# The first group's projections between the latents' statistics and their broadcasts, in a hybrid MLA/SSD decoder layer

## What is computed

```python
h = rmsnorm(x, g_pre_mix)
h_q, h_kv, h_pe, z, xbc_raw, dt_raw, gate_a, gate_b = split(h @ w_in)
# latent attention
cq, c_kv = rmsnorm(h_q, g_q), rmsnorm(h_kv, g_kv)        # 384 and 256 latents
q = cq @ w_uq;  k_nope = c_kv @ w_uk;  v = c_kv @ w_uv   # per head
o_attn = attend(q, rope(h_pe), k_nope, v)
# SSD branch
xbc = silu(b_conv + sum_k full[:, k:k+s] * w_conv[k])    # causal, 4 taps
dt  = softplus(dt_raw + dt_bias);  la = -exp(a_log) * dt
decay = exp(cumsum(la) differences);  state = state * decay + B (x dt)
o_ssm = rmsnorm_per_group((C state + d_skip x) * silu(z)) * g_ssm
x = x + rmsnorm((sig(gate_a)*(o_attn @ w_a) + sig(gate_b)*(o_ssm @ w_b)) @ w_out)
x = x + rmsnorm(relu(rmsnorm(x) @ w_up)**2 @ w_down)
```

## Time and profile of the kernel before

| | us |
|---|---|
| median of 3 runs | 1641.25 |
| range | 1639.22 to 1641.71 |
| the profiled execution | 1638.68 |
| its span in the trace | 1636.8 |
| mean granted PE clock, share of full | 0.951 |
| PE busy | 1474.2 |
| DVE busy | 871.0 |
| ACT busy | 528.0 |
| POOL busy | 586.5 |

### The profile page before, as it was taken

The page is one execution under the profiler, slowest core; times in us unless marked ns, Lnnn a source line. Parts: engine busy times, 40 slices in busy tenths (PEclk is TensorE's granted clock), DMA queues, the critical chain, the costliest instruction groups (busy, mean ns, idle before and its releaser), DMA issues.

```text
span 1636.8 us, 29300 instructions
## 1 busy us (share of the span) xinstructions
PE 1474.2 (90%) x11936; PEld 1365.1 (83%) x11936; DVE 871.0 (53%) x1735; ACT 528.0 (32%) x1026; POOL 586.5 (36%) x748
## 2 busy tenths in 40 slices
PE   4989999999999999999976889999957999999995
PEld 4989788898988889888864668789957999999994
DVE  5574687877878777786874322213344222222225
ACT  3232343424344343434423222222223333222221
POOL 1443252342524334142310222234443444444451
PEclk9888999999999999999987889999977999999997
DMA  3223222222223222222220698733311232222221
GB/s 118 65 69 94 83 79 78 83 76 82 73 77 88 80 78 74 84 85 65 83 90 4 186 292 267 240 113 117 104 39 52 94 97 83 95 98 91 91 91 65
DMA packets 109590, 160.51 MB, mean 98 GB/s; under 512 B 16497, under 2 KB 83569, under 8 KB 109457
## 3 DMA queue, kind: packets, MB, share of 16 engines
q1 hardware_dynamic: 56592, 130.14, 24.9%
q10 hardware_dynamic: 52864, 28.51, 6.0%
HBM read 145.87 MB, written 12.74 MB: 97 GB/s over the span
## 4 chain that ended last, share of the span: by engine, by line
PE 62%; DVE 25%; issue 4%; ACT 4%; ACTq 2%; SPq 1%; POOL 1%; DMA 1%; DVEq 0%; POOLq 0%
PE lin L456 51%; PE Pb L589 2%; DVE arena L1313 2%; PE lin L645 2%; ACTq L1061 2%; DVE arena L1312 2%; DVE arena L1314 1%; DVE arena L1311 1%; DVE sm L1384 1%; PE Pb L487 1%; PE lin L495 1%; DVE arena L1419 1%; ACT arena L970 1%; DVE arena L1319 1%; PE Pb L748 1%
## 5 line engine op out<-in xcount | busy, mean ns | idle before, releaser
L413 POOL TENSOR_TENSOR w_lo<-w_stage,w_hi 128x256 fp32r<-128x256 f32 x736 | 574.4, 812 | 1002.9 <-ACT w_hi L849 1002.9
L456 PE MATMUL lin<-act_hi,w_hi 128*128 128x260 f32 x1760 | 371.2, 293 | 19.7 <-DVE acc L1580 8.6
L456 PE MATMUL lin<-act_lo,w_hi 128*128 128x260 f32 x1760 | 360.4, 287 | 0.0
L456 PEld LDWEIGHTS lin<-act_hi,w_hi 128*128 128x128 f32 x1760 | 277.6, 194 | 29.4 <-issue 22.0
L456 PEld LDWEIGHTS lin<-act_lo,w_hi 128*128 128x128 f32 x1760 | 278.6, 194 | 0.0
L849 ACT ACTIVATE w_hi<-w_stage 128x1024 fp32r<-128x1024 f32 x184 | 193.7, 1053 | 247.1 <-PE lin L456 229.3
L456 PE MATMUL lin<-act_hi,w_lo 128*128 128x260 f32 x1760 | 234.6, 286 | 0.0
L456 PE MATMUL lin<-mid_hi,w_hi 128*128 128x260 f32 x1024 | 211.3, 288 | 14.3 <-DVEq L1499 6.2
L456 PEld LDWEIGHTS lin<-act_hi,w_lo 128*128 128x128 f32 x1760 | 220.8, 190 | 3.3 <-issue 3.3
L456 PE MATMUL lin<-mid_lo,w_hi 128*128 128x260 f32 x1024 | 207.7, 285 | 0.0
L456 PEld LDWEIGHTS lin<-mid_hi,w_hi 128*128 128x128 f32 x1024 | 159.7, 191 | 21.1 <-issue 12.7
(11 more groups left out here) (238 smaller groups left out, 1906.8 us busy)
## 6 DMA issues: line engine op xcount, KB each, us to landing
w_stage<-in_wall SPq DMA_DIRECT2D x184, 512.0 KB, 3.7
arena<-in_cache SPq DMA_DIRECT2D x124, 144.0 KB, 3.2
arena<-in_state ACTq DMA_DIRECT2D x16, 512.0 KB, 5.3
out_stateT<-arena ACTq DMA_DIRECT2D x16, 512.0 KB, 4.0
o_attn<-in_cache SPq DMA_DIRECT2D x64, 128.0 KB, 3.6
o_attn<-in_cache ACTq DMA_DIRECT2D x64, 128.0 KB, 3.9
arena<-in_xT SPq DMA_DIRECT2D x8, 520.0 KB, 5.8
out_yT<-arena SPq DMA_DIRECT2D x8, 260.0 KB, 2.1
```

The lines of the kernel that those rows point to most:

```text
L413: low = pool.tensor_tensor(w_lo[:, slot, part], w_stage[:, slot, part], w_hi[:, slot, part].bitcast(F32), ALU.subtract)
L456: mm = pe.matmul(lin[:, pl.slot, hf, 0:HALF], w[:, ch.slot, off:off + P], r[:, hf * HALF:(hf + 1) * HALF], start=(k == 0 and p == 0), stop ...
```

## The change

On every engine the same work is put in another order, and two pieces are done otherwise.

- PE: the statistics of the latents now follow projection x0; the transposes for the scan (`scan_rows`) and the query latents' broadcast (`bcq`) follow x1; the key/value latents' broadcast (`bckv`) follows c. `bcq` and `bckv` move from `PRE_LIN` into `FIRST_LIN`, so the two slots of `lin` are taken in the new order.
- DVE: `softplus` comes behind all five latent copies. The convolutions of group 0 come behind the key latents, in the order c, x0, x1, b (`FIRST_CONV`), since c's accumulator is the one that does not lie over `sq`; the second waits for the DMA that writes the latents out. Between them stand the z gates, the copies of the decays and `queries_out`.
- Sample decays: DVE multiplies a diagonal with the 32 x 16 numbers (`sdec_rhs`, into `diag_flat`), and PE spreads all 512 columns with one matmul instead of 32.
- ACT: the DMAs of the convolution's history and of group 0's sample state are issued behind the eight roundings of the normalised input, ahead of the rounding of chunk 1. The rounding of the latents goes between the evacuations of group 0.

The diff, cut to its core:

```diff
-FIRST_LIN = IN_LIN + ["uq0", "uq1", "uk", "uv", "ql"]
+FIRST_LIN = ["x0", "x1", "bcq", "b", "c", "bckv", "z0", "z1", "uq0", "uq1", "uk", "uv", "ql"]
+FIRST_CONV = [3, 0, 1, 2]
-PRE_LIN = ["bcx", "misc", "q0", "q1", "q2", "kv0", "kv1", "bcq", "bckv"]
+PRE_LIN = ["bcx", "misc", "q0", "q1", "q2", "kv0", "kv1"]
...
-            pe.wait_ge(S["cs_ready"], 1)
...
-            tr.then_inc(S["rows_tr"], 1)
...
-            pe.wait_ge(S["lat_sq"], 3)
-            statistics(Pb[0:TOKT, 2, 8:16], sq[:, 0:3, :], 3).then_inc(S["stat_done"], 1)
-            pe.wait_ge(S["lat_sq"], 5)
-            statistics(Pb[0:TOKT, 0, 0:8], sq[:, 3:5, :], 2).then_inc(S["stat_done"], 1)
-            pe.wait_ge(S["rstd_diag"], 2)
-            broadcast_stat(fixed(7))
-            pe.wait_ge(S["rstd_diag"], 3)
-            broadcast_stat(fixed(8))
+            def scan_rows():
+                pe.wait_ge(S["cs_ready"], 1)
+                for c in range(NCH):
+                    pe.transpose(Pb[:, 3, 32 * c:32 * c + 32], cs3[:, CHUNK * c:CHUNK * (c + 1)], ident[0:32, 0:32])
+                for c in range(NCH):
+                    tr = pe.transpose(Pb[:, 3, 128 + 32 * c:160 + 32 * c], dtw[0:32, 0, CHUNK * c:CHUNK * (c + 1)],
+                                      ident[0:32, 0:32])
+                tr.then_inc(S["rows_tr"], 1)
+
+            def latent_statistics():
+                pe.wait_ge(S["lat_sq"], 3)
+                statistics(Pb[0:TOKT, 2, 8:16], sq[:, 0:3, :], 3).then_inc(S["stat_done"], 1)
+                pe.wait_ge(S["lat_sq"], 5)
+                statistics(Pb[0:TOKT, 0, 0:8], sq[:, 3:5, :], 2).then_inc(S["stat_done"], 1)
...
                 if not has_rest:
-                    for name in IN_LIN:
-                        project(name)
-                    pe.wait_ge(S["cs_ready"], 1)
-                    pe.wait_ge(S["sp_ln"], 2)
-                    for f in range(GROUPS):
-                        for h in range(HPG):
-                            mm = pe.matmul(Pb[:, 1, 64 * f + 16 * h:64 * f + 16 * h + 16],
-                                           ident[0:32, 4 * f + h:4 * f + h + 1].to_broadcast([32, P]),
-                                           cs3[:, SEQ:SEQ + 16], start=True, stop=True)
-                    mm.then_inc(S["sdec_mm"], 1)
+                    project("x0")
+                    latent_statistics()
+                    project("x1")
+                    scan_rows()
+                    pe.wait_ge(S["rstd_diag"], 2)
+                    broadcast_stat(c_lin(0, "bcq"))
+                    project("b")
+                    project("c")
+                    pe.wait_ge(S["rstd_diag"], 3)
+                    broadcast_stat(c_lin(0, "bckv"))
+                    project("z0")
+                    project("z1")
+                    pe.wait_ge(S["sdec_rhs"], 1)
+                    pe.matmul(Pb[:, 1, :], ones[0:32, :], diag_flat[0:32, 0:SSM_HEADS * 16], start=True, stop=True
+                              ).then_inc(S["sdec_mm"], 1)
                     pe.wait_ge(S["act_ready"], KT + 5)
                     queries(0)
                     queries(1)
...
+            act.dma_start(raw[:, :, SAMP0:RAWW], d["hist"][0]).then_inc(S["hist_in"], 16)
+            for t in range(2):
+                act.dma_start(sS[:, t], d["state"][:, 2 * t:2 * t + 2, :, :].rearrange("b h p n -> (h p) b n")
+                              ).then_inc(S[f"st_in{t}"], 16)
...
-            for k in range(5):
-                act.wait_ge(S["norm_val"], KT + k + 1)
-                act.activation(mid_hi[:, k, :], sq[:, k, :], ACT.Copy).then_inc(S["norm_hi"], 1)
-            act.dma_start(o["kvT"], sq[:, 3:5, :]).then_inc(S["kv_out"], 16)
-            act.dma_start(o["kpeT"], Kt[64:96, 0, :]).then_inc(S["kpe_out"], 16)
-            act.wait_ge(S["cs_ready"], 1)
-            act.activation(cs3[:, SEQ + 8:SEQ + 16], dtw[0:32, 0, SEQ:T], ACT.Exp, scale=ahead[:, :]
-                           ).then_inc(S["sp_ln"], 1)
-            act.wait_ge(S["kv_out"], 16)
-            act.wait_ge(S["rows_ready"], 1)
+            def latents_rounded(first, last):
+                for k in range(first, last):
+                    act.wait_ge(S["norm_val"], KT + k + 1)
+                    act.activation(mid_hi[:, k, :], sq[:, k, :], ACT.Copy).then_inc(S["norm_hi"], 1)
...
-                def conv_tanh(k):
-                    act.wait_ge(S["conv_acc"], i * 4 + (k + 1))
+                def conv_tanh(n):
+                    k = n if has_rest else FIRST_CONV[n]
...
-                    history()
-                    for k in range(4):
-                        raw_evac(k)
-                        if k:
-                            conv_tanh(k - 1)
-                    for k in range(2):
-                        round_chunk(c_chunk(i, f"z{k}").next())
-                        z_evac(k)
-                    conv_tanh(3)
+                    raw_evac(0)
+                    act.wait_ge(S["cs_ready"], 1)
+                    act.activation(cs3[:, SEQ + 8:SEQ + 16], dtw[0:32, 0, SEQ:T], ACT.Exp, scale=ahead[:, :]
+                                   ).then_inc(S["sp_ln"], 1)
+                    raw_evac(1)
+                    latents_rounded(0, 3)
+                    raw_evac(2)
+                    raw_evac(3)
+                    latents_rounded(3, 5)
+                    act.dma_start(o["kvT"], sq[:, 3:5, :]).then_inc(S["kv_out"], 16)
+                    act.dma_start(o["kpeT"], Kt[64:96, 0, :]).then_inc(S["kpe_out"], 16)
+                    round_chunk(c_chunk(i, "z0").next())
+                    z_evac(0)
+                    act.wait_ge(S["kv_out"], 16)
+                    conv_tanh(0)
+                    round_chunk(c_chunk(i, "z1").next())
+                    z_evac(1)
+                    conv_tanh(1)
                     conv_rows_out()
-                    state_in()
+                    conv_tanh(2)
                     round_chunk(c_chunk(i, "UKV"))
                     queries_out(0)
                     queries_out(1)
+                    conv_tanh(3)
                     round_chunk(c_chunk(i, "UKV").next())
                     keys_out()
+                    act.wait_ge(S["rows_ready"], 1)
                     return
...
                 dve.tensor_copy(cols(lat[:, k, :]), lin_cols(fixed(2 + k))).then_inc(S["lin_free"], 1)
-                if k == 1:
-                    softplus()
...
+            softplus()
...
+            def scan_rows():
+                dve.wait_ge(S["rows_tr"], 1)
+                dve.tensor_scalar(rows[:, 0, :, :].rearrange("p c h -> p (c h)"), Pb[:, 3, 0:128], -1.0, None, ALU.mult)
+                dve.tensor_copy(rows[:, 1, :, :].rearrange("p c h -> p (c h)"), Pb[:, 3, 128:256]
+                                ).then_inc(S["rows_ready"], 1)
+                dve.wait_ge(S["sp_ln"], 2)
+                dve.tensor_tensor(diag_flat[0:32, 0:SSM_HEADS * 16].rearrange("p (h c) -> p h c", c=16),
+                                  spread(ident[0:32, 0:32], 16), repeat(cs3[:, SEQ:SEQ + 16], SSM_HEADS), ALU.mult
+                                  ).then_inc(S["sdec_rhs"], 1)
...
-                    for k in range(4):
-                        raw_samples(k)
-                        if k:
-                            silu(k - 1)
-                        conv(k)
+                    link(dve.memset(raw[:, :, 0:3], 0.0))
+                    raw_samples(0)
+                    dve.wait_ge(S["stat_done"], 2)
+                    inverse_rms(Pb[0:TOKT, 2, 8:16], 1.0 / Q_LORA, S["rstd_diag"])
+                    raw_samples(1)
+                    query_latents()
+                    dve.wait_ge(S["stat_done"], 3)
+                    inverse_rms(Pb[0:TOKT, 0, 0:8], 1.0 / KV_LORA, S["rstd_diag"])
+                    raw_samples(2)
+                    raw_samples(3)
+                    key_latents()
+                    scan_rows()
+                    conv(0)
+                    dve.wait_ge(S["kv_out"], 16)
+                    conv(1)
                     z_gate(0)
-                    z_gate(1)
-                    silu(3)
+                    silu(0)
                     dve.wait_ge(S["sdec_mm"], 1)
                     for h in range(2):
                         src = Pb[64 * h:64 * h + 64, 1, :].rearrange("p (f t h c) -> p f t h c", f=GROUPS, t=2, h=2)
                         cp = dve.tensor_copy(sdec_all[64 * h:64 * h + 64, :, :, :], src[:, :, :, h, :])
                     cp.then_inc(S["sdec_ready"], 1)
                     dve.wait_ge(S["sdec_ready"], 1)
+                    conv(2)
+                    z_gate(1)
+                    silu(1)
+                    queries_out(0)
+                    queries_out(1)
+                    conv(3)
+                    silu(2)
                     for t in range(2):
                         scaled_state(t)
-                    queries_out(0)
-                    queries_out(1)
                     keys_out()
+                    silu(3)
                     latents_out()
```

58 lines of the change are left out of this document (21 added, 37 removed).

## The result

The changed kernel takes 1626.07 us (median of 8 runs, 1619.58 to 1632.3), the kernel before in the same comparison 1641.48 (8 runs, 1638.44 to 1647.7). The measured ratio is 0.9896, interval 0.9877 to 0.9915: 17.1 us less, 14.0 to 20.2. The two medians themselves are 15.4 apart. A second measurement gave 0.9883 (0.9862 to 0.9904), with medians 16.7 apart. The forecast was 12.3 less, 1629.0. By the ratio, 1641.25 x 0.9896 = 1624.2 lies just under the lower end of the range, 1625.0; the median itself, 1626.07, lies just above that end. The profiled execution took 1627.35, with a span of 1625.2 and a mean granted clock of 0.952.

The account below looks back on a forecast made before the run. PE bounds the kernel (62% of the chain), with DVE 25%. Group 1's matmul moves from 148.71 to 133.7, 15.0 earlier, less 0.9 and 1.8 of clock, 12.3: 1641.25 becomes 1629.0 us, range 1625.0 to 1634.5.

Parts of the forecast that it names:

- no stop ahead of kv1: On PE before projection kv1: the 3.10 us wait for DVE's latent copy, queued behind the softplus, disappears.
- no wait for a chunk in b, c or z0: Group 0 projections: ACT's rounding stays on time; otherwise the stops return, gain 0 to 3 us, chance 0.04.
- no wait for `kv_out`: Before DVE's second convolution: the latents' write-out is done by 109, DVE asks at 111, so hidden by 2 us.
- the stops of 3 and 4 on PE: PE waits for DVE about 3 us between the two query products and about 4 ahead of group 1.
- half clock in group 1's start: Group 1's `on_all` and x0 start at half clock, costing 1.8 us, bounds 0 and 3.5.
- the path from the end of kv0 to `on_all`: PE 39.9 us to `bckv`, then DVE 31.4 to the last silu; 0.9 added for queries possibly at half clock.
- of it the statistics: PE's latent statistics between x0 and x1, priced at 6.7 us from the trace of the kernel before.
- of it the four convolutions: Group 0's convolutions on DVE behind `bckv`: 14.4 us, POOL beside them half the time, bounds 12.0 and 18.0.
- The decays' 10.38 goes altogether: Group 0 on PE: the 32 tiny decay matmuls' 10.38 us vanishes; the replacing matmul, 1.1, lies on no path.
- Cost nothing: Early history and state DMAs take 3.3 us on ACT, delaying chunk 1's rounding, with 0.7 of cover before q0.
- Last convolution ending before 129: Group 0 on DVE: the last convolution ending before 129 or after 133 would show the forecast wrong.
- behind group 1's x0 there is only a shift: After group 1's x0: instructions are the same before and after; any difference other than a shift would show the forecast wrong.

Follow-up runs that it names:

- one convolution less: The changed kernel with the four taps of group 0's last convolution left out (output wrong), median 1624.75 us, ratio 0.9905 to the kernel before.
- the state moved: The changed kernel with the two multiplications scaling the sample state put behind the last silu and the keys; median 1624.83 us, ratio 0.9893 to the kernel before.
- the second trace of after: The changed kernel profiled and measured once more, unchanged; median 1627.15 us, ratio 0.9883 to the kernel before.
- its second trace: The kernel before profiled and measured once more, unchanged; median 1645.65 us, ratio 1.001.
- the two kernels of its order with the product: The kernel before with one matmul spreading the sample decays, 1644.05 us, ratio 1.0005; the same plus early history and state DMAs, 1630.55 us, ratio 0.9935.
- the late state DMAs: The changed kernel with history's DMA behind chunk 1's rounding and state's DMAs behind z1's evacuation; median 1626.39 us, ratio 0.9906 to the kernel before.
- values-first kernel: The changed kernel with the value products ahead of the keys' projection in every group; median 1628.58 us, ratio 0.9934 to the kernel before.
- a ninth: The changed kernel with both latent roots made together and x0's convolution ahead of the key latents; median 1628.79 us, ratio 0.9908 to the kernel before.

## Why the forecast was right in kind and short in size

**Right.** The place and the mechanism: no stop ahead of kv1; x1 slow, from 78.11 to 85.5 some 7.4, with a granted clock of 0.57 over 78 to 82; no wait for a chunk in b, c or z0; no wait for `kv_out`; the stops of 3 and 4 on PE; half clock in group 1's start, 1.5 for 1.8. DVE's chain is the bound: one convolution less gives 2.2, the state moved gives 0.4 and turns into a wait for ACT. No run puts the statistics and the broadcasts back in front of group 0, so what the stop of 7.30 alone was worth is not shown; 9.1 is what the whole new order gives beyond the product and the DMAs (77.2 to 68.1), and in that order the place of the softplus alone is worth 6.8.

**The step that failed is a size in the sum:** the path from the end of kv0 to `on_all`, put at 39.9 + 31.4 = 71.3 and another 0.9 for half clock in the queries. It measured 68.1, with no half clock in the query products. Its terms, with what they measured in the first trace of after:

| term | predicted | measured |
|---|---|---|
| start of the part, end of kv0 | 62.42 | 61.91 |
| PE from there to the end of `bckv` | 39.9 | 37.9 |
| of it the statistics | 6.7 | 4.84 |
| DVE from there to the last silu | 31.4 | 30.0 |
| of it the four convolutions | 14.4 | 13.9 |
| of it waiting in hand-overs | 1.0 | 0.2 |
| half clock in the queries | 0.9 | 0 |
| half clock in group 1 | 1.8 | 1.5 |

The start and the two stretches add up to 0.5 + 2.05 + 1.4 = 4.0, less 0.3 between the last silu and the matmul: that is the 3.7 by which 18.7 is over 15.0. With the 0.9 and 0.3 of clock that did not come, 12.3 turns into 17.2, the lead at the start of group 2. The largest single term is the statistics, 1.9 of it. The 6.7 had been read behind the stop of 3.10, which this very change removes, and the granted clock over that stretch was 0.70; in after it was 1.00 (stretch):

```profile
73.30:78.10 4.80, 4.80 (x83) 4.80 (x81) 4.70 (x4) 1.94 (x3) 0.04 (x1) 1.00 0.34 109
```

The price should have had a bound at full clock. How much of it is the single execution's, the others show: 4.84 three times, and 4.89, 4.94, 5.19, 5.37, 5.4 and 6.91, in kernels with the same order up to there. The 6.91, at a clock of 0.66, came with no stop ahead of it, so the price behind the stall was no upper bound either. The four convolutions at 14.4 are also not what the prediction's words give: POOL there "half of the time" makes 15.0, and 14.4 is 40%, its three splits of 4.3 in the 31.4. In the second trace of after the path was 70.4 long, 39.4 + 31.0, against 71.3 + 0.9 predicted. The forecast fits that execution to 1.8, and the first to 4.1.

**The edits' own values were partly wrong, though their sum was near.** "The decays' 10.38 goes altogether" is true on PE, but alone it is worth 1.5 to 2.4, since the state's DMA came next. "Cost nothing" for the early DMAs holds with the new order (0.0, the history only a rounding later), and hides that with the old one they bring 6.6 to 7.6. The ACT queue's price was also high: the state's two issues took 1.26, not 2.59.

```profile
33.46 0.67 ACTq L866 DMA_DIRECT2D arena<-in_hist  x1
34.16 1.26 ACTq L868 DMA_DIRECT2D arena<-in_state  x2
35.47 1.06 ACT L854 ACTIVATE w_hi<-w_stage 128x1024 fp32r<-128x1024 f32 x1 [1.38 <-issue]
```

**Margins.** The softplus was done at 80.5 and PE asked at 85.4: 4.9, where I had 6 and had named 5 as the sign. The first root took 5.0, not 3.4, and ended at 85.64, 0.4 ahead of `bcq` where I had 3. The second root took 7.0 (91.37 to 98.42), not 3.4, because eight of its 65x8 operations took 0.59 to 0.75 instead of 0.16 while POOL was splitting (91.75 to 97.48). It ended 0.2 ahead of the broadcast that reads it. This was the nearest rival of all, and I had not priced it. The Trainium skill says in "SBUF — State Buffer", section "SBUF: two separate sides", that a VectorE operation with two SBUF inputs or in a two-port mode and a GpSimd one take the shared ports for a whole instruction each, and that the loser is blocked. These rows agree in kind, with 0.5 for an operation of 0.16, more in proportion than the taps' 0.35 on 0.79.

**A sign that was set wrongly.** "Last convolution ending before 129" was named as a sign against me, and it ended at 124.99. By my own sum it would have ended near 128.8 (133.7 less the state, keys and two silus, 4.9), so the lower bound left no room for a chain that is only shorter.

**The other assumption that failed** is that behind group 1's x0 there is only a shift. In the first two traces the lead falls from 17.2 to 11.0 over groups 2 to 5, and each step is a loss of clock of 1.5. These two executions are 11.3 apart; that this is near the 12.3 forecast is luck: the part ahead of group 2 gained more, and the groups behind it lost what I had not counted. The medians differ by 15.4 and, the second time, by 16.7 (by the ratios 17.1 and 19.2), nearer to what the part ahead of group 2 gives alone, 17.2. If groups 2 to 5 always cost after 6 more than before, they could hardly stand so far apart. The first trace of before was one without losses in the groups; its second trace has one, and the two kernels of its order with the product have five and three. So the losses do not belong to the changed order alone. That over many executions both kernels lose alike is argued from the medians, not shown: only profiled executions have a trace, and three of the changed order (the late state DMAs' among them) show four losses at the same places. Whether the new start makes them more frequent stays open. The values-first kernel's three do not settle it either, since the number differs between two executions of before.

**The range** was too narrow on one side. It held the unknown costs of the edit and not what an execution does by itself: identical code behind group 8 took 803 to 812 in 14 traces, and the same kernel ran from 1619.6 to 1632.3. The base was sound, 1641.25 for a median that came out at 1641.48. The median of after is 2.9 from the forecast, 0.2% of the time; it is the gain that was short, 12.3 for 15.4 by the medians and 17.1 by the ratio.

**A better kernel** was not found. The scaled state last stands at 0.9893, the same as after within its interval. To gain more, the written latents, the place of the decays' product and ACT's list have to move along with a convolution.

## What to carry to other kernels

A stall removed by an edit can take its clock loss with it (the statistics took 4.84 to 5.4 in eight traces, but 6.91 in a ninth): price what follows it at full clock as one bound, and do not carry over the duration read behind the stall alone. Ask for each edit what is late next *in the order it is put in*: the same product was worth 1.5 to 2.4 in one order and 9.1 in the other, and the early DMA of the state, with the history's, 6.6 to 7.6 in the one, alone 0.0 in the other. And before reading two traces of a long kernel against each other, cut them at places with identical code behind; what differs there (here 681 against 688) is not yet the edit's.

## What the runs showed of the hardware

- Identical groups take 97.25 or 98.8, with the granted clock at 1.00 throughout or at 0.50 for some 4 us, behind 24 products of 128 columns and six of 16, and in the kernel with the values first behind the 24 alone. PE was busy 4.79 of the 5.00 ahead of the fall at 314, with a stop of 0.88 just before these. The Trainium skill names idle gaps in "TensorE: Matmul & The Clock Gate", section "HAM oscillation — how this bites in real kernels"; the trace agrees with that behind the stops (0.54 at 126 to 130, where PE was busy 1.34 of 4), and shows besides that a fall can come behind narrow work with no stop longer than 0.9. That the narrow work causes it is not shown: the same rows stand in groups that kept the clock. Once it came, it mostly came again in the next groups, some 99 apart.
- The time of an execution follows its mean granted clock: the eight runs of after go from 1619.58 at 0.958 to 1632.3 at 0.948, 1.3 for each 0.001, and one such loss is 1.5.
- Issuing the same pair of DMAs (the state's two) on ACT's queue took 2.59 in one place (at 127.76 in before) and 1.26 in another (at 34.16 in after), and 1.35 in a third (at 112.38 in the kernel with the late state DMAs).
- The inverse root of a 65x8 mean, with its diagonal, took 3.1 on DVE with POOL idle (86.40 to 89.46 in before) and 7.0 with POOL splitting beside eight of its operations (91.37 to 98.42 in after).
